# Moving the key half of a memory projection to the start of a fused two-block kernel

## The reference, cut to what matters

```python
# first block
sh, sc, gt = split(silu(c) @ w_mod + b_mod, 3)         # "modulation"
h  = rmsnorm(x, pre_g) * (1 + sc) + sh                  # 512 rows
hc = rmsnorm(ctx, pre_g) * (1 + sc_c) + sh_c            # 256 rows
q, k, v, gates... = h @ w_in ;  k_c, v_c = hc @ w_in[:, K_OFF:V_END]
x  = x + gt * rmsnorm(mixer(...) @ w_o, post_g)
# second block
x  = x + hybrid_mixer(rmsnorm(x, g_mix), w_in_2, ...)
k, v = split(rmsnorm(mem_2, g_mem_kv) @ w_kv_mem, 2)    # 256 rows x 2048
q  = rmsnorm(x, g_mem_q) @ w_q_mem
x  = x + softmax(q @ k.T / 16) @ v @ w_o_mem
x  = x + relu(rmsnorm(x, g_mlp) @ w1) ** 2 @ w2
out = rmsnorm(x, g_final)
```

## Time and profile before

| | |
|---|---|
| median of 3 runs | 1725.44 us (1724.52 to 1729.97) |
| profiled execution, first to last instruction (its span) | 1727.8 us |
| PE busy in it | 1685.5 us, 98% of the span |
| DVE, ACT, POOL busy | 884.8, 772.0, 631.1 us |
| mean TensorE clock granted, over the span | 0.992 of full speed |
| first matmul of phase V | 42.11 us |
| first matmul of phase MKV | 787.92 us |
| first matmul of phase V2 | 847.29 us |

### The profile page before, as it was taken

One profiled execution on the slowest core, in us unless ns is written; L12 is line 12 of the kernel. 1 busy time (PEld: TensorE's weight loads), 2 busy tenths in 40 slices (PEclk: granted clock), 3 DMA queues, 4 the chain that ended last, 5 costly groups with the idle time before them and its releaser, 6 DMA issues. The chain is left out here.

```text
span 1727.8 us, 27062 instructions
## 1 busy us (share of the span) xinstructions
PE 1685.5 (98%) x10190; PEld 1431.6 (83%) x10190; DVE 884.8 (51%) x1554; ACT 772.0 (45%) x1366; POOL 631.1 (37%) x439
## 2 busy tenths in 40 slices
PE   7999999999999999999999999999999999999998
PEld 6987777778888889988997788798787788989896
DVE  4223333344445328947645565687544575555552
ACT  5324554532223334556545655444445324626251
POOL 1007665633330076742103422866200227414242
PEclk9999999999999999999999999999999999999999
DMA  7231221223334223243731111223511223222221
GB/s 318 100 96 37 73 79 49 73 104 121 109 111 146 98 73 118 103 162 134 290 130 65 52 47 50 85 104 133 216 50 50 98 73 114 107 98 97 97 98 49
DMA packets 29800, 181.65 MB, mean 105 GB/s; under 512 B 3352, under 2 KB 5784, under 8 KB 10112
## 3 DMA queue, kind: packets, MB, share of 16 engines
q1 hardware_dynamic: 22136, 150.12, 24.0%
q10 hardware_dynamic: 7560, 30.09, 4.9%
HBM read 169.57 MB, written 10.50 MB: 104 GB/s over the span
## 5 line engine op out<-in xcount | busy, mean ns | idle before, releaser
L409 PE MATMUL acc<-rarena,wh 128*128 128x512 f32 (+1 forms) x1720 | 659.1, 383 | 10.5 <-DVE farena L1863 2.8
L410 PE MATMUL acc<-rarena,wh 128*128 128x512 f32 (+1 forms) x1720 | 643.7, 374 | 0.0
L411 PE MATMUL acc<-rarena,wl 128*128 128x512 f32 (+1 forms) x1720 | 643.5, 374 | 0.0
L409 PEld LDWEIGHTS acc<-rarena,wh 128*128 128x128 f32 x1720 | 324.7, 189 | 91.9 <-issue 26.7
L411 PEld LDWEIGHTS acc<-rarena,wl 128*128 128x128 f32 x1720 | 324.6, 189 | 62.8
L410 PEld LDWEIGHTS acc<-rarena,wh 128*128 128x128 f32 x1720 | 324.9, 189 | 56.8 <-issue 0.5
L312 DVE TENSOR_TENSOR wl<-raw,wh 128x2048 fp32r<-128x2048 f32 x85 | 207.0, 2435 | 259.5 <-ACT wh L306 259.4
L306 ACT ACTIVATE wh<-raw 128x2048 fp32r<-128x2048 f32 x103 | 196.5, 1908 | 76.2 <-PE acc L411 69.4
L312 POOL TENSOR_TENSOR wl<-raw,wh 128x2048 fp32r<-128x2048 f32 x18 | 82.6, 4586 | 153.2 <-ACT wh L306 153.2
L2495 POOL TENSOR_TENSOR wl<-raw,wh 128x512 fp32r<-128x512 f32 x78 | 104.9, 1373 | 91.5 <-ACT wh L1281 91.5
L487 PE MATMUL acc<-wh,rarena 128*128 128x256 f32 x384 | 109.1, 284 | 4.0 <-DVE rarena L1738 2.5
(11 more groups left out here) (320 smaller groups left out, 2904.2 us busy)
## 6 DMA issues: line engine op xcount, KB each, us to landing
raw<-in_w SPq DMA_DIRECT2D x129, 1024.0 KB, 4.8
early<-in_wmod SPq DMA_DIRECT2D x8, 1024.0 KB, 19.7
farena<-in_gate ACTq DMA_DIRECT2D x4, 1024.0 KB, 4.7
mkv_scratch<-rarena ACTq DMA_DIRECT2D x2, 2048.0 KB, 12.5
rarena<-mkv_scratch ACTq DMA_DIRECT2D x1, 4096.0 KB, 13.3
farena<-in_rpb ACTq DMA_DIRECT2D x16, 240.0 KB, 3.8
farena<-in_x_grid SPq DMA_DIRECT2D x2, 1024.0 KB, 8.0
o_scratch<-early ACTq DMA_DIRECT2D x8, 256.0 KB, 2.0
```

The costliest lines, as they stand in the source:

```text
L409: mm(o, w[0], m[0], start=start, stop=False)
L410: mm(o, w[0], m[1], start=False, stop=False)
L411: return mm(o, w[1], m[0], start=False, stop=stop)
```

## The change

1. PHASES: the four key jobs become phase MK, ahead of phase V. Phase MV keeps the four value jobs at the old place. SP's queue now brings the memory rows and two MK jobs first; ACT starts the loads of the next four jobs (`load_early`).
2. In the opening the memory rows are normalised first, then each key group stands between steps of the opening. The key pairs are written to `mk_out` and from there to `mkv_dram`; the pair `hm0` is written to a new `hm_dram` (2 MB) and read back at phase WO into the old place of `hm`.
3. The squares of context and tokens are taken by three wide ACT instructions instead of sixteen, and DVE halves them. The low parts of `hc` and the splits of all four MK jobs and the first V job are POOL's.
4. In the middle the whole preparation of the memory rows is gone. `x1_tile` 0 stands at group 2 of job 2 of MV, tiles 1 to 4 at each of the next four groups, tiles 5 to 7 after the phase. POOL makes half of two splits (`split_half`) and all of V2's first. The second column sum and the spread of `rcol` stand behind the first groups of V2.

```diff
-PHASES = [("V", 4, 24), ...  ("WO", 4, 8), ("MKV", 8, 16), ("FL", 1, 1), ...
+PHASES = [("MK", 4, 8), ("V", 4, 24), ...  ("WO", 4, 8), ("MV", 4, 8), ("FL", 1, 1), ...
-X1_TILES = {1: (0,), 2: (1, 2), 3: (3,), 4: (4, 5), 5: (6,), 6: (7,)}
+X1_TILES = {(1, 1): 0, (2, 0): 1, (2, 1): 2, (3, 0): 3, (3, 1): 4}
+X1_AFTER = range(5, KT)
+EARLY_JOBS = 6
...
+            sp.dma_start(mem, A["mem"]).then_inc(s_("mem_in"), 16)
+            load_job(0)
+            load_job(1)
             sp.dma_start(ctx0, A["ctx"]).then_inc(s_("ctx_in0"), 16)
...
+            memory_keys(0, None)
+            pe.wait_ge(s_("pair_summed"), 1)
+            column_sums(S[1], sqm[:, 0], 2, True, True).then_inc(s_("acc0_done"), 1)
+            memory_keys(1, lambda: spread_root(0))
+            pe.wait_ge(s_("pair_summed"), 2)
+            column_sums(S[0], xsq[0][:, 0], 4, True, True).then_inc(s_("acc0_done"), 1)
+            pe.wait_ge(s_("silc_ready"), 4)
+            chunk_rows(0)
+            chunk_rows(1)
+            spread_root(1)
+            memory_keys(2, lambda: chunk_columns(0))
+            chunk_rows(2)
+            chunk_rows(3)
+            memory_keys(3, lambda: chunk_columns(1))
+            for n in (4, 5, 6):
+                chunk_rows(n)
+            chunk_columns(2)
+            chunk_rows(7)
+            chunk_columns(3)
...
+            token_hi(1)
+            row_copy(6)
             ctx_hi(2)
+            row_copy(7)
+            token_hi(2)
             ctx_hi(3)
...
-            act.dma_start(mem, A["mem"]).then_inc(s_("mem_in"), 16)
+            act.dma_start(hm_rows[1], hm_dram).then_inc(c_("hm_back"), 16)
...
+            v.wait_ge(s_("sqm_ready"), 1)
+            link(halve(sqm, 4))
+            halve(sqm, 2).then_inc(s_("accm_done"), 1)
+            v.wait_ge(s_("rmsm_ready"), 1)
+            link(nc.vector.reciprocal(rstd_m, rstd_m))
+            for k in range(KT + 1):
+                if k < KT:
+                    stt(mem[:, k], mem[:, k], vec(P_MKV + k), rstd_m, MUL, MUL).then_inc(s_("hmf_ready"), 1)
+                if k > 0:
+                    v.wait_ge(s_("hm_hi"), k)
+                    lo(hm0[1][:, k - 1], mem[:, k - 1], hm0[0][:, k - 1]).then_inc(s_("hm_ready"), 1)
...
+                    if (c, t) in X1_TILES:
+                        x1_tile(X1_TILES[c, t])
+                    if c > 1 and t == 0:
+                        hold(v, "half_split", c - 1)
+                        split_half(nc.vector, JB["MV"] + c + 1, 1, s_("lo_done"))
+                    v.wait_ge(s_("mkv_hi"), 8 + 2 * c + t + 1)
```

More of the change, by code:

```diff
@@ L94, in build @@
             pass
+        with nc.sbuf_tensor("below", [128, 80 * 256], f32):
+            with nc.sbuf_tensor("edge", [128, 16 * 256], f32) as edge:
+                pass
         with nc.sbuf_tensor("lower", [128, 64 * 256], f32):
@@ L510, in _, with spread_root, chunk_rows @@
             pe.wait_ge(s_("consts_ready"), 5)
[L511 to L523, removed]
+            pe.wait_ge(s_("accm_done"), 1)
+            for k in range(2):
+                last = mm(S[1][:, 0:CTX], ones[:], sqm[:, k], start=k == 0, stop=k == 1)
+            last.then_inc(s_("summ_done"), 1)
+            def spread_root(x):
+                pe.wait_ge(s_("ncol_ready"), x + 1)
+                spread((S[1], S[0])[x], (ncol_c, ncol)[x], (2, 4)[x])
+            def chunk_rows(n):
                 pe.wait_ge(s_(f"wmod_in{n}"), 16)
@@ L843, in _ @@
             last.then_inc(s_("acc_ready"), 1)
-            pe.wait_ge(s_("ncol_ready"), 4)
-            spread(S[0], rcol, 4)
             for c in range(4):
@@ new lines, in _ @@
+            f(sqm, mem, ACT.Square).then_inc(s_("sqm_ready"), 1)
+            split_hi(act, 0, 2, 0)
+            act.wait_ge(s_("consts_ready"), 4)
+            act.wait_ge(s_("summ_done"), 1)
+            f(rstd_m, S[1][:, 0:CTX], ACT.Sqrt, scale=1.0 / D, bias=eps).then_inc(s_("rmsm_ready"), 1)
+            split_hi(act, 0, 2, 1)
+            for k in range(KT):
+                act.wait_ge(s_("hmf_ready"), k + 1)
+                f(hm0[0][:, k], mem[:, k], ACT.Copy).then_inc(s_("hm_hi"), 1)
+                if k == 2:
+                    load_early(2)
@@ new lines, in _ @@
+            act.wait_ge(s_("ctx_in0"), 16)
+            f(sqm, ctx0, ACT.Square).then_inc(s_("sq0_ready"), 1)
+            keys_hi(0, 0)
+            act.wait_ge(s_("hm_ready"), KT)
+            token_squares(0)
+            keys_hi(0, 1)
+            root(0)
+            token_squares(1)
+            load_early(3)
+            split_hi(act, 0, 2, 2)
+            keys_hi(1, 0)
+            keys_hi(1, 1)
+            root(1)
+            row_copy(0)
+            row_copy(1)
+            split_hi(act, 0, 2, 3)
@@ new lines, in _ @@
+            load_early(4)
+            keys_hi(2, 0)
+            for t in range(2):
+                wait_evacuated(act, 0, 2, GB["MK"] + 2 + t)
+            act.dma_start(mkv_dram[:, 0:4096].rearrange("p (x n) -> p x n", x=2)[:, :, 0:1024],
+                          rarena[:, 96 * 256:104 * 256].bitcast(f32).rearrange("p (x n) -> p x n", x=2))\
+               .then_inc(c_("mk_spilled"), 16)
+            keys_hi(2, 1)
+            ctx_hi(0)
+            row_copy(2)
+            row_copy(3)
+            token_hi(0)
@@ L1111, in _ @@
+            act.dma_start(hm_dram, hm_rows[0]).then_inc(c_("hm_spilled"), 16)
             with act.Fori(0, 2) as it:
@@ L1140, in _ @@
             split_hi(act, 0, 2, JB["QK"] + 1)
+            hold(act, "hm_spilled", 32)
             def rope_hi(it, pc, x):
@@ L2657, in _layout @@
     gate = square(np.asarray(i["w_mod"][0])[:, 2 * D:])
-    jobs = _pair_cols(win, seq(48, 4))
+    memory = square(i["w_kv_mem_2"][0], 8)
+    jobs = memory[:4] + _pair_cols(win, seq(48, 4))
     jobs += _pair_cols(win, [(32 + p, 40 + p) for p in range(8)])
@@ L2665, in _layout @@
     jobs += oc + oa + [w for pair in zip(ga, gb) for w in pair]
-    jobs += square(i["w_o"][0]) + square(i["w_kv_mem_2"][0], 8)
+    jobs += square(i["w_o"][0]) + memory[4:]
     fl = np.zeros((KT, 128, JW), np.float32)
```

331 lines of the change are left out of this document (164 added, 167 removed).

## The result

The changed kernel takes **1748.8 us** (median of 4 runs, 1746.5 to 1751.8), the kernel before in the same job 1726.6 (1724.5 to 1730.0). The ratio is 1.013, 95% interval [1.0114, 1.0147]: 22 us slower. Three executions of the kernel before that took 1825 us and more, in a slower state, are left out of every median and ratio. The forecast was 1737, range 1721 to 1747: the direction was right, the size half of what came. The profiled execution has a span of 1750.1, mean granted clock 0.985, against 1727.8 before.

The account below looks back on a forecast made before the run. PE, busy in 98% of the span, was taken as the bound. Opening +24, phase WO -1.5, middle -12.3 and clock +1.5 gave +11.7: span 1739.5, or 1737 us on the runs' median; range 1721 to 1747.

Parts of the forecast that it names:

- the charge of nothing for DVE beside POOL: Opening: DVE's scaling beside POOL's splits costs nothing extra, since one earlier split took 2.29 us beside POOL against 2.28.
- a rival with 0.14: Whole kernel slower still, 1746 to 1752: low clock through the key groups, +14, or the DVE/POOL port lock; chance 0.14.
- the list: Program order on each engine with row lengths plus 0.1 us per hand-over; DVE scales from 15.7, phase V starts at 65.1.
- PE's row without a gap from 28.5: Opening: from 28.5 us PE works in one unbroken row of key groups, chunks, columns, sums and spreads to 55.0.
- while that cover lasts: Opening: POOL's splits, 4.54 us each, are ready 1 to 2 us ahead of PE, so they cost nothing.
- Phase WO, -1.5: Phase WO: the memory norm goes, with one PE wait of 1.1 us and two matmuls of some 0.4; -1.5 us.
- The middle, -12.3: Middle: eight key groups leave; V2's third group begins 52.7 us after MV's first matmul, before 65.0; -12.3 us.
- +1.5 for the clock: Middle: FL's idle stretches may lower the clock for FL and V2's first group, 0 to 4.5 us, taken as +1.5.
- the lock step of tile and bank: Middle: splits, tiles and bank emptying form a closed chain of 9.3 us a job, where PE has 5.7 of work.
- rival B: Whole kernel unchanged, 1724: opening costs its low bound, 19, and the middle's tiles overlap better, -19.3; chance 0.17.
- The +1.0 for V's first groups: Start of phase V: its first group waits for the last context tile, raising the opening's cost from +23.0 to +24.
- The transfers at nothing: Opening and phase WO: 5 MB more queued ahead of V, keys written out and the 2 MB read-back cost no time.

## Why the prediction was wrong

**The step that failed is the charge of nothing for DVE beside POOL.** The prediction read the earlier trace rows: the DVE split at 759.39 takes 2.29 beside POOL from 759.43, so there is no lock. But DVE was first, by 0.04 us. The one who comes second waits, and that was POOL. Only DVE's length was looked at. The first of POOL's seven instructions, taken by itself, and the view of all seven (least, median and greatest length in ns) show it:

```profile
759.43 2.85 POOL L2550 TENSOR_TENSOR farena<-farena,early 128x256 f32<-128x256 f32 x1
```

```profile
L2550 POOL TENSOR_TENSOR farena<-farena,early x7: 732/737/2847, 759.4 to 766.8; 128x256 f32<-128x256 f32 x7
```

It takes 2.85 where 0.74 is usual, and ends 0.6 after DVE's split. A row where POOL is first stood in the prediction's own list: the eight scaled tiles of the earlier trace rows take 5.37, and two of them are blocked.

```profile
L2057 DVE SCALAR_TENSOR_TENSOR farena<-farena,par x8: 471/473/1554, 775.8 to 779.7; 128x256 f32<-128x256 f32 x8
```

```profile
775.79 1.28 POOL L2550 TENSOR_TENSOR farena<-farena 128x512 f32<-128x512 f32 x1 [4.43 <-ACT farena L1369]
779.37 1.52 POOL L2550 TENSOR_TENSOR farena<-farena 128x512 f32<-128x512 f32 x1 [2.29 <-ACT farena L1369]
```

The first tile starts at 775.80, 0.01 behind POOL, and takes 1.55; the last starts at 779.66, inside POOL's second instruction, and takes 1.52. About 2.1 of the 5.37 us are the lock. A third place is in the timeline of DVE and POOL around 617 us,

```profile
617.85 4.51 DVE L312 TENSOR_TENSOR wl<-raw,wh 128x2048 fp32r<-128x2048 f32 x1 [8.91 <-ACT wh L306]
...
617.82 2.39 POOL L2509 TENSOR_TENSOR early<-rarena 128x1024 f32<-128x1024 f32 x1
```

where POOL's instruction is 0.03 ahead, and in the view of that line on DVE:

```profile
L312 DVE TENSOR_TENSOR wl<-raw,wh x85: 2277/2293/4515, 52.9 to 1694.7; 128x2048 fp32r<-128x2048 f32 x85
```

A greatest length of twice the median, for an instruction of one shape, was the sign. The prediction priced the lock at +4.6 and put it in a rival with 0.14. The Trainium skill (SBUF — State Buffer, Who interferes with whom) says that a DVE instruction with two inputs in SBUF contends with a GpSimd instruction that reads SBUF, and that whoever issues first has the shared port pair for the whole instruction while the other blocks; the runs agree (4.2 us twice beside whole splits, 0.5 beside pieces of 0.89).

**The opening's other steps.** DVE begins to scale at 16.18 against 15.7 in the list (PE's sum took 2.04 where 1.7 was taken), and the first key matmul is at 21.8; where no split stood beside it, at 17.6 to 18.6. The key groups followed the tiles at 0.73 per tile, faster than the 1.0 of the list, which had the lock of the earlier trace rows in it. The errors cancel: 64.3 against 65.1. What PE's row without a gap from 28.5 hid is that POOL's splits were charged at nothing "while that cover lasts", for PE; the one who paid was DVE. The pause that followed put the clock down a second time, which the list had only at the start.

**Phase WO, -1.5, was 0.4.** The wait of 1.1 in the earlier trace rows was charged to the norm of the memory rows. It is the third group of phase WO itself (753.82 in the trace of before) that waits for ACT to empty the first group's bank, and it stands in the changed kernel, at 783.61, with the same 1.1. The name of the releasing line said so: L1369 empties a WO bank. From WO's first matmul to that of the memory projection it is 46.6 us before and 46.2 now.

**The middle, -12.3 and +1.5 for the clock, was -9.4 in all.** FL starts 32.2 us after MV, earlier than the list's last bank at 34.7, waits longer for its tiles, and its last tile begins at 41.8 (list: FL ends at 43.5). V2's third group is at 55.6 where 52.7 and 1.5 had been forecast: 1.4 off. The 34.7 is a slip of the list: 16.5 and two rounds of 9.3 give 35.1. Of the 6 us that the prediction called waits in the kernel before, its trace shows 3.8. The mechanism was right, and the runs sharpen it: not the lock step of tile and bank (emptying the bank first made it worse by 5) but the way over POOL's half split, and DVE's idle time in front of banks. The lock was missing here too: the 0.4 and 1.05 us of the two half splits are as much as the 1.4 of the miss, though no run separates them from the clock. Better overlap of the tiles, which rival B had, is what two edits made of it, 46.8.

**The sum.** On the span +22.3 against +11.7: 5.8 in the opening with V's first group, 1.1 in phase WO, 1.4 in the middle, and 2.3 behind it. The +1.0 for V's first groups didn't come: from V's first matmul to WO's it is 699.2 us in both kernels. Behind V2's third group the order is the same everywhere, and the fourteen profiles have 874.7 to 877.4 us there, so those 2.3 can't be put down to the change. The transfers at nothing hold: no wait of PE on a chunk or on the read-back shows.

**The chances.** Slower had 0.67 and was right. The time lies 1.8 us above the range. The case that came, the lock, was in the text with its price of 4.6 for the one place where it was looked for; there were two in the opening and two small ones in the middle.

## What to carry to other kernels

Before work is put beside work of another engine, look for the pair of engines in both orders, and read the length of the one that came second; the view of a line with its least, median and greatest length finds it in one look. A blocked instruction waits for what is left of the blocker, so split a long POOL instruction into pieces, or give it to DVE in a row where DVE waits anyway. Where PE pauses, count the pause and, as a risk, the matmuls behind it at the low clock, and mend such pauses first: here one of 2.25 us was worth 3.9 at the start of phase V and 3.0 in the total.

## What the runs showed that was not expected

**DVE was not blocked where one of its two inputs was in PSUM.** In the changed kernel DVE scales the tokens with a PSUM operand from 47.65, the first instruction before and the others beside POOL's split from 48.52, all at 0.61 per instruction (4.87 / 8), as before beside the split of the earlier trace rows:

```profile
47.65 4.87 DVE L1891 TENSOR_TENSOR farena<-farena,S 128x512 f32<-128x512 f32 x8 [3.51 <-PE S L523]
...
48.52 4.61 POOL L326 TENSOR_TENSOR wl<-raw,wh 128x2048 fp32r<-128x2048 f32 x1 [8.45 <-ACT wh L320]
```

**The same pause doesn't always cost clock.** At the start of phase QK PE waits 2.77 to 2.85 us in every kernel of this family. In the changed kernel the granted clock behind it is 0.50 and 0.70 (the wait's row in PE's timeline, then the windows):

```profile
160.24 0.76 PE L429 MATMUL acc<-rarena,wh 128*128 128x512 f32 x1 [2.78 <-DVE farena L1941]
```

```profile
160.00:164.00 4.00, 3.77 (x9) 3.02 (x10) 0.09 (x1) 1.11 (x4) 2.75 (x3) 0.50 0.00 0
164.00:168.00 4.00, 4.00 (x16) 2.83 (x15) 0.42 (x1) 1.79 (x1) 3.10 (x5) 0.70 0.00 0
```

In the kernel with the splits on DVE the same wait is followed by windows at full clock:

```profile
151.74 0.48 PE L429 MATMUL acc<-rarena,wh 128*128 128x512 f32 x1 [2.78 <-DVE farena L1944]
```

```profile
152.00:156.00 4.00, 4.00 (x18) 3.02 (x17) 0.42 (x1) 1.58 (x4) 2.98 (x4) 1.00 0.00 0
156.00:160.00 4.00, 3.10 (x16) 2.15 (x16) 1.66 (x5) 2.25 (x4) 3.45 (x6) 1.00 0.00 0
```

Ten of the fourteen profiled runs lost clock there and four did not. What decides it stays open. From the end of that wait to phase WO the order is the same everywhere; the four profiles that kept the clock take 607.6 to 607.8 us there, the other ten 607.9 to 610.8. That is why landmarks inside a span, and not the spans alone, were compared above. The Trainium skill (TensorE: Matmul & The Clock Gate, Why this matters for your kernels) says that gaps between bursts bring the lower clock back; that held behind the pauses of the changed kernel's opening (0.51 and 0.50), but behind this wait and the one of 2.25 us only in part of the runs.
